# Sampled rows' convolution and layer norm taken out of the prompt's, and the cached rows' and bias copies' DMAs reordered

## What is computed

```python
def conformer_layer(x, conv_prev, g_pre, w_in, conv_w, conv_b, ln_g, ln_b, w_out, g_post):
    h = rms_norm(x, g_pre)
    a, b, z = jnp.split(h @ w_in, 3, axis=-1)
    glu = a * jax.nn.sigmoid(b)
    full = jnp.concatenate([conv_prev.astype(glu.dtype), glu], axis=1)
    c = lax.conv_general_dilated(full, conv_w[:, None, :].astype(glu.dtype), (1,), 'VALID',
                                 dimension_numbers=('NWC', 'WIO', 'NWC'),
                                 feature_group_count=D_INNER) + conv_b
    y = jax.nn.silu(layer_norm(c, ln_g, ln_b)) * jax.nn.silu(z)
    return x + rms_norm(y @ w_out, g_post), full[:, -(CONV_W - 1):]
```

## Time and profile before

| what | value |
| --- | --- |
| median of three runs | 1080.82 us |
| the profiled execution's own time | 1079.11 us |
| its span, first to last instruction | 1077.0 us |
| TensorE matmuls busy | 972.6 us, 90% |
| VectorE busy | 527.9 us, 49% |
| ScalarE busy | 419.5 us, 39% |
| GpSimd busy | 273.2 us, 25% |
| granted TensorE clock, mean | 0.972 of full speed |

### The profile page before, as it was taken

How to read it: one execution, slowest core, us unless ns; L and a number is a source line. 1 busy time by engine, 2 the same in 40 slices (tenths; PEclk the granted TensorE clock), 3 DMA queues, 4 the chain that set the end, 5 groups by cost and what they waited for, 6 DMA issues and landing times. The chain is left out here.

```text
span 1077.0 us, 16750 instructions
## 1 busy us (share of the span) xinstructions
PE 972.6 (90%) x6142; PEld 806.0 (75%) x6142; DVE 527.9 (49%) x1443; ACT 419.5 (39%) x864; POOL 273.2 (25%) x303
## 2 busy tenths in 40 slices
PE   2899999994699999998998999999999999899994
PEld 2799999652358878876998888788788887786652
DVE  3399999972331440223111445645545546445653
ACT  4466666432421121211222454555545536323320
POOL 0378888430130000002000132323233224200000
PEclk9999999997699999999998999999999999899997
DMA  8246333277301042035542212212211005703310
GB/s 222 64 115 180 97 97 107 104 288 258 105 8 46 40 147 69 23 83 128 138 93 55 49 36 60 59 40 60 59 41 40 21 1 125 211 20 119 120 50 29
DMA packets 153815, 97.12 MB, mean 90 GB/s; under 512 B 94004, under 2 KB 141780, under 8 KB 153655
## 3 DMA queue, kind: packets, MB, share of 16 engines
q1 hardware_dynamic: 142894, 81.52, 28.1%
q10 hardware_dynamic: 10105, 9.50, 2.7%
q0 software_dynamic: 736, 5.05, 1.2%
HBM read 87.22 MB, written 18.85 MB: 98 GB/s over the span
## 5 line engine op out<-in xcount | busy, mean ns | idle before, releaser
L1506 PE MATMUL psum<-arena 128*128 128x256 f32 (+3 forms) x928 | 195.2, 367 | 3.2 <-issue 2.6
L675 ACT ACTIVATE arena<-psum 128x512 f32<-128x512 f32 (+10 forms) x225 | 90.4, 453 | 260.4 <-PE psum L1826 72.5
L1506 PEld LDWEIGHTS psum<-arena 128*128 128x128 f32 (+2 forms) x928 | 160.5, 187 | 31.6 <-issue 10.1
L1526 PE MATMUL psum<-u_hi,tile_hi 128*128 128x288 f32 x512 | 158.2, 309 | 3.6 <-DVE kept L1282 3.6
L1527 PE MATMUL psum<-u_lo,tile_hi 128*128 128x288 f32 x512 | 152.3, 297 | 0.0
L1528 PE MATMUL psum<-u_hi,tile_lo 128*128 128x288 f32 x512 | 152.1, 297 | 0.0
L654 POOL TENSOR_SCALAR arena<-arena,kept 128x128 f32<-128x128 f32 (+3 forms) x128 | 76.6, 608 | 211.6 <-DVE kept L1354 211.6
L1158 DVE SCALAR_TENSOR_TENSOR psum<-arena,psum 128x512 f32<-128x512 f32 x168 | 125.7, 748 | 0.0
L1526 PE MATMUL psum<-h_hi,tile_hi 128*128 128x288 f32 x384 | 115.0, 299 | 10.0 <-ACT arena L675 4.3
L1527 PE MATMUL psum<-h_lo,tile_hi 128*128 128x288 f32 x384 | 114.6, 298 | 0.0
L1528 PE MATMUL psum<-h_hi,tile_lo 128*128 128x288 f32 x384 | 113.8, 296 | 0.0
(11 more groups left out here) (239 smaller groups left out, 1490.1 us busy)
## 6 DMA issues: line engine op xcount, KB each, us to landing
tile_whole<-in_b_w_in SPq DMA_DIRECT2D x64, 256.0 KB
tile_whole<-in_a_w_in SPq DMA_DIRECT2D x24, 512.0 KB
arena<-in_cmp_w SPq DMA_DIRECT2D x3, 2048.0 KB, 9.9
arena<-in_w_kv SPq DMA_DIRECT2D x6, 1024.0 KB, 7.7
bias_copies<-bias_line SPq DMA_DIRECT2D x4, 1280.0 KB
arena<-in_x_prompt SPq DMA_DIRECT2D x8, 512.0 KB, 16.2
arena<-in_a_w_out SPq DMA_DIRECT2D x4, 1024.0 KB, 29.3
arena<-bias_copies SPq DMA_DIRECT2D x16, 256.0 KB, 3.9
```

What stands on the lines that cost most here:

```text
L675: return nc.scalar.activation(out, in_, ACT.Copy, scale=scale)
L1506: ins = pe.matmul(out, l, r, start=(k == 0), stop=(k == len(pairs) - 1))
L1526: pe.matmul(out, w_hi[:, k], h, start=(k == 0), stop=False)
```

## The change

The sampled rows leave the prompt's chain. In the convolution VectorE does only the prompt's 22 taps and the final sum. Behind its adds GpSimd multiplies, for each block and each half of the sequences, the sliding windows by the 31 taps (16 products of 4 x 8 x 31 elements, three buffers), and VectorE sums each over the taps (16 reductions: 8 behind the centring, 8 behind the prompt's scaling). Then the bias, and the sampled rows' own mean, centring, square, variance, root, reciprocal, scaling and Silu for all blocks together. The prompt's multiplication by Silu(z) moves from GpSimd to VectorE. TensorE makes six of the eight mean matmuls before compression 0 and the other two behind it, at 512 columns. On SP the bias copies leave chunk C_OA, and at C_KV - 1 the order becomes: weights of compression 1, cached rows 12 to 15, the prompt's rows, the sampled rows, a wait for the sample's sums (whose buffers lie where the first kv chunks go). The strip bs is loaded at C_Q, its four copies on VectorE move behind q_ready. The bias copies are issued by ScalarE between the conv outputs' stores and the load of gpost_a. Three semaphores are merged into others. Core of the diff:

```diff
-CONV = 2 * W_ON + W_OFF + 2
+CONV = W_ON + 1
...
-                if c == C_OA:
-                    sp.wait_ge(S["line_out"], 16)
-                    for h0 in range(0, H, 4):
-                        sp.dma_start(bias_copies[h0:h0 + 4], bias_dram[h0:h0 + 4].unsqueeze(1).broadcast_to([4, P, NX])).then_inc(S["line_out"], 16)
+                if c == C_KV - 1:
+                    sp.wait_ge(S["cs_mm"], 2)
+                    sp.dma_start(w1_sb, I["cmp_w1"][1].rearrange("(j p) n -> p j n", p=P)).then_inc(S["w1_in"], 16)
+                    for n in range(12, 16):
+                        past_cmp(n)
                     sp.wait_ge(S["proj_a"], C_OA)
                     for t in range(4):
                         sp.dma_start(x_sb[:, t], I["x_prompt"][0, t * P:(t + 1) * P, :]).then_inc(x_in[t], 16)
-                if c == C_KV - 1:
-                    sp.wait_ge(S["cs_mm"], 2)
-                    sp.dma_start(w1_sb, I["cmp_w1"][1].rearrange("(j p) n -> p j n", p=P)).then_inc(S["w1_in"], 16)
                     sp.wait_ge(S["conv_step"], CONV * KD)
                     sp.dma_start(x_sb[0:NS, 4], I["x_sample"].rearrange("b t d -> (b t) d")).then_inc(x_in[4], 16)
+                    sp.wait_ge(S["sample_sums"], 2 * KD)
+                if c == C_Q:
                     sp.wait_ge(S["line_out"], 80)
                     sp.dma_start(bs, bass.AP(bias_copies.tensor, SEQ - 1 - PAST, [[P * NX, H], [NX - 1, DS], [1, KS]])).then_inc(S["bs_in"], 16)
-                    for n in range(12, 16):
-                        past_cmp(n)
...
-            pool.wait_ge(S["z_ready"], KD)
-            for m in range(KD):
-                pool.wait_ge(S["lns_ready"], m + 1)
-                pool.tensor_tensor(out=zA[:, m], in0=conv[:, m], in1=zA[:, m], op=ALU.mult).then_inc(S["y_ready"], 1)
+            pool.wait_ge(S["state_ready"], 16)
+            pool.wait_ge(S["glu_ready"], 3 * KD)
+            for n in range(2 * KD):
+                m, half = n // 2, n % 2
+                if n >= 3:
+                    pool.wait_ge(S["sample_sums"], n - 2)
+                new = glu_s[:, m, 4 * half:4 * half + 4]
+                windows = bass.AP(new.tensor, new.offset, [new.ap[0], [DS + W - 1, 4], [1, DS], [1, W]])
+                taps = vecT[:, m, 0:W].unsqueeze(1).unsqueeze(1).broadcast_to([P, 4, DS, W])
+                pool.tensor_tensor(out=sample_prod[:, n % 3].rearrange("p (b t) w -> p b t w", b=4), in0=windows, in1=taps,
+                                   op=ALU.mult).then_inc(S["sample_terms"], 1)
...
+            act.wait_ge(S["stat_mm"], 1 + KD)
+            act.wait_ge(S["centred"], KD + 1)
+            nc.scalar.activation(sg[:, 0, 0:KD * NS].rearrange("p (m n) -> p m n", m=KD), conv[:, :, SEQ:NT], ACT.Square).then_inc(S["sqd"], 1)
+            act.wait_ge(S["eps_ready"], 2)
+            nc.scalar.activation(rstd_ln[:, SEQ:NT], rstd_ln[:, SEQ:NT], ACT.Sqrt).then_inc(S["std_ready"], 1)
+            act.wait_ge(S["lnx_ready"], KD + 1)
+            for m in range(KD):
+                normed_silu(m, slice(SEQ, NT))
 
...
                 act.dma_start(O["conv_sample"][0, b, W - 1 - DS:W - 1], conv_out_s[DS * b:DS * b + DS]).then_inc(S["co_out"], 16)
+            act.wait_ge(S["line_out"], 16)
+            for h0 in range(0, H, 4):
+                act.dma_start(bias_copies[h0:h0 + 4], bias_dram[h0:h0 + 4].unsqueeze(1).broadcast_to([4, P, NX])).then_inc(S["line_out"], 16)
             act.dma_start(gpost_a, I["a_norm_post"][0:1, :].broadcast_to([P, D])).then_inc(S["gpost_in"], 16)
...
                     if w == 0:
                         V.tensor_scalar(acc_p, glu_p[:, m, 0:SEQ], tap, bias, ALU.mult, ALU.add).then_inc(S["conv_step"], 1)
-                        V.tensor_scalar(on, new[:, :, 0:DS], tap, bias, ALU.mult, ALU.add).then_inc(S["conv_step"], 1)
                     else:
-                        dve.wait_ge(S["conv_step"], before + tap_step(w - 1) + 1)
+                        dve.wait_ge(S["conv_step"], before + w)
                         V.scalar_tensor_tensor(out=acc_p, in0=glu_p[:, m, w:w + SEQ], scalar=tap, in1=acc_p,
                                                op0=ALU.mult, op1=ALU.add).then_inc(S["conv_step"], 1)
-                        dve.wait_ge(S["conv_step"], before + tap_step(w - 1) + 2)
-                        V.scalar_tensor_tensor(out=on, in0=new[:, :, w:w + DS], scalar=tap, in1=on,
-                                               op0=ALU.mult, op1=ALU.add).then_inc(S["conv_step"], 1)
-                    if w < W_OFF:
-                        far = W_ON + w
-                        tap = vecT[:, m, far:far + 1]
-                        if w == 0:
-                            V.tensor_scalar(late, new[:, :, far:far + DS], tap, None, ALU.mult).then_inc(S["conv_step"], 1)
-                        else:
-                            dve.wait_ge(S["conv_step"], before + tap_step(w - 1) + 3)
-                            V.scalar_tensor_tensor(out=kept_s if w == W_OFF - 1 else late, in0=new[:, :, far:far + DS], scalar=tap,
-                                                   in1=late, op0=ALU.mult, op1=ALU.add).then_inc(S["conv_step"], 1)
-                dve.wait_ge(S["conv_step"], before + CONV - 2)
-                V.tensor_tensor(out=kept_s, in0=kept_s, in1=on, op=ALU.add).then_inc(S["conv_step"], 1)
+                dve.wait_ge(S["conv_step"], before + W_ON)
                 dve.wait_ge(S["term_added"], (W_OFF - 1) * (m + 1))
                 V.tensor_tensor(out=conv[:, m, 0:SEQ], in0=acc_p, in1=tap_sum, op=ALU.add).then_inc(S["conv_step"], 1)
+
+            def sample_sum(n):
+                m, half = n // 2, n % 2
+                dve.wait_ge(S["sample_terms"], n + 1)
+                V.tensor_reduce(conv[:, m, SEQ + 32 * half:SEQ + 32 * half + 32], sample_prod[:, n % 3], AX.X,
+                                ALU.add).then_inc(S["sample_sums"], 1)
 
...
+            for n in range(KD):
+                sample_sum(n)
...
+            for n in range(KD, 2 * KD):
+                sample_sum(n)
+            conv_s = conv[:, :, SEQ:NT]
+            dve.wait_ge(S["sample_sums"], 2 * KD)
+            V.tensor_tensor(out=conv_s, in0=conv_s, in1=vecT[:, :, W + 1:W + 2].broadcast_to([P, KD, NS]), op=ALU.add).then_inc(S["sample_sums"], 1)
+            dve.wait_ge(S["z_ready"], KD)
+            for m in range(KD):
+                dve.wait_ge(S["lns_ready"], m + 1)
+                V.tensor_tensor(out=zA[:, m, 0:SEQ], in0=conv[:, m, 0:SEQ], in1=zA[:, m, 0:SEQ], op=ALU.mult).then_inc(S["y_ready"], 1)
 
...
+            dve.wait_ge(S["stat_mm"], KD + 2)
+            dve.wait_ge(S["sample_sums"], 2 * KD + 1)
+            V.tensor_tensor(out=conv_s, in0=conv_s, in1=pb(2, NS).unsqueeze(1).broadcast_to([P, KD, NS]),
+                            op=ALU.subtract).then_inc(S["centred"], 1)
+            dve.wait_ge(S["stat_mm"], KD + 3)
+            V.tensor_scalar(rstd_ln[:, SEQ:NT], pb(3, NS), EPS, None, ALU.add).then_inc(S["eps_ready"], 1)
+            dve.wait_ge(S["std_ready"], 2)
+            link(dve, V.reciprocal(rstd_ln[:, SEQ:NT], rstd_ln[:, SEQ:NT]))
+            dve.wait_ge(S["sqd"], KD + 1)
+            V.tensor_tensor(out=conv_s, in0=conv_s, in1=rstd_ln[:, SEQ:NT].unsqueeze(1).broadcast_to([P, KD, NS]),
+                            op=ALU.mult).then_inc(S["lnx_ready"], 1)
+            dve.wait_ge(S["lns_ready"], 2 * KD)
+            V.tensor_tensor(out=zA[:, :, SEQ:NT], in0=conv_s, in1=zA[:, :, SEQ:NT], op=ALU.mult).then_inc(S["y_ready"], 1)
...
+            pe.wait_ge(S["ones_ready"], 1)
+            pe.wait_ge(S["glu_ready"], 3 * KD)
+
+            def mean_part(m):
+                pe.wait_ge(S["conv_step"], CONV * (m + 1))
+                return pe.matmul(pb(0, SEQ), ones, conv[:, m, 0:SEQ], start=(m == 0), stop=(m == KD - 1))
+
+            for m in range(KD - 2):
+                mean_part(m)
             compress(0)
+            mean_part(KD - 2)
+            mean_part(KD - 1).then_inc(S["stat_mm"], 1)
             pe.wait_ge(S["w2_in"], 16 * 8)
             pe.wait_ge(S["hid_ready"], 2)
             product(pb(4, 480), ((w2_sb[:, 0, ht], hid[:, ht]) for ht in range(2))).then_inc(S["kc_mm"], 1)
...
+            pe.wait_ge(S["sample_sums"], 2 * KD + 1)
+            for m in range(KD):
+                ins = pe.matmul(pb(2, NS), ones, conv[:, m, SEQ:NT], start=(m == 0), stop=(m == KD - 1))
+            ins.then_inc(S["stat_mm"], 1)
             pe.wait_ge(S["hid_ready"], 4)
             pe.wait_ge(S["z_ready"], KD)
             for b in range(DB):
                 ins = product(pb(4, DB, P, p1=60)[:, b], ((hid[:, ht, 60 * b:60 * b + 60], w2_sb[:, 1, ht]) for ht in range(2)))
             ins.then_inc(S["vc_mm"], 1)
+            pe.wait_ge(S["sqd"], KD + 1)
+            for m in range(KD):
+                ins = pe.matmul(pb(3, NS), ones, sg[:, 0, m * NS:(m + 1) * NS], start=(m == 0), stop=(m == KD - 1))
+            ins.then_inc(S["stat_mm"], 1)
...
+                if t == 4:
```

(44 more changed lines are left out.)

34 lines of the change are left out of this document (15 added, 19 removed).

## The result

The changed kernel takes 1098.54 us (median of four runs, 1096.95 to 1101.69) against 1080.32 for the kernel before (1079.29 to 1080.88): a ratio of 1.0173, 95% interval 1.0148 to 1.0199. It is slower by some 18 us. The forecast was 1103 with a range of 1083 to 1114. The profiled execution took 1099.36 us, with a span of 1097.5, which is 20.5 above the span before; its granted clock is 0.960 in the mean.

What follows compares the result with a forecast made beforehand. TensorE, busy nine tenths or more except near 240 to 290 us, was taken as the bound. The profiled 1079.11 plus 22.6 (late third output tile and clock) plus 0.6 gave 1102.3, stated as 1103, range 1083 to 1114.

Steps and rivals of the forecast that it cites:

- Step 1: Prompt's convolution alone: VectorE blocks every 19 to 20 us instead of 22.32, compression 0 ends at 229.5; gain 2 us.
- Step 2: Cached rows: first load at 240 (bounds 233 and 250), compression 1 starts at 261, ends 22.7 us earlier.
- Step 3: Sampled rows' sums and own norm around compression 1: output rows start at 303.5, 17.4 us won up to there.
- the sign of step 3 being wrong: Output rows starting over 15 us behind compression 1's end; 13 us was forecast.
- Step 4: Bias copies on ScalarE hold it and the gain's load, landing at about 360; third output tile and clock: 22.6 us late.
- The spell at the lower clock: TensorE, empty some 36 us after two output tiles, loses 2.5 to 3 us more at half clock.
- Step 5: Small things: the sample's bias column copies moved to just before the head blocks, 0.6 us lost.
- the copies cost nothing on ScalarE: Rival: ScalarE's queue takes the bias copies at some 0.4 us each, gain's load overtakes them; 1064, faster; chance 0.14.
- only the issue blocks: Rival: gain lands with the queue's release at 340 to 344, third tile at 353.5; 1085; chance 0.10.
- The late chain: Rival: sampled rows' windows at double price, or cached rows starting at 250; 1112; chance 0.10.

Runs made afterwards that it cites:

- Experiment 5: The kernel before with only experiment 4's DMA order, sampled rows left in the prompt's convolution and norm: 1071.23 us, ratio 0.9902.
- experiment 6: Experiment 5 with GpSimd's two DRAM to DRAM copies moved behind its multiplications by Silu(z): 1057.52 us, ratio 0.9776.
- Experiment 8: experiment 4 with conv output transposes ahead of the sample's variance, ScalarE's sample root and Silus behind stores and gain's load: 1053.34 us, ratio 0.9741.
- experiments 1: The changed kernel with the four bias copies put back on SP, early, at chunk C_OA: 1071.07 us, ratio 0.9914.
- experiment 2: The changed kernel with the gain's load issued ahead of the four bias copies, still on ScalarE: 1084.15 us, ratio 1.0038.
- experiment 3: The changed kernel with the bias copies in the same place, 128 copies outermost instead of 4 heads: 1064.01 us, ratio 0.9856.
- experiment 4: The changed kernel with the bias copies in old shape on SP, late, behind the sampled rows' load: 1060.47 us, ratio 0.9820.
- experiment 7: The kernel before with the bias copies at their old place on SP, 128 copies outermost: 1070.36 us, ratio 0.9899.

## Why the prediction was right, and where it was off

The mechanism that the prediction called decisive is the one that the runs show. That the forecast, 1103, comes within 5 us of the median, 1098.54, is also owed to errors that cancel, as the steps tell.

**Step 1** held. The blocks follow each other in 19.0 to 20.0 us (19 to 20 predicted), the last block's sum starts at 213.69 (predicted 214), compression 0 ends at 228.23 (229.5).

**Step 2** had the right mechanism and one wrong term: I let the weights of compression 1 be held until 240, as three weight chunks were held for 26.36 us before. They are one DMA and their issue took 0.37 us; they landed 14.0 us later, at 242.3, but the cached loads behind them were issued without waiting for that. The first came at 232.75, which was my lower bound, and compression 1 started at 254.81, six us earlier than the 261 forecast; it ended at 283.28, 7.2 earlier. The distance between the two, taken as 21.1, was 22.1. Experiment 5 shows that GpSimd's copies do hold cached loads when they run at the same time (23.67 against 7.86 in experiment 6). Here they were issued at 209.70 and landed at 234.0, about when the cached loads began.

**Step 3** held in its prices: a product 2.1 us (2.3), a reduction 1.19 (1.2), the eight scalings of the prompt 4.91 (4.9). The last sum starts at 276.79 and ends 8 us before my 286. But the chain behind compression 1 was undersized: the output rows start 15.6 us behind its end, not 13, which is over the 15 that the prediction itself named as the sign of step 3 being wrong. I had given its links no prices of their own. One that I had left out is 3.9 us long: the sampled rows are centred at 285.74, but their square on ScalarE starts at 289.63, behind the copy of the product for the values (1.02 us from 288.71), which stands ahead of it in ScalarE's program. Experiment 8 measures what the chain costs against one that is off TensorE's path: 7 us at the second tile's end (329.56 against 322.62).

**Step 4**, which the prediction called the one that decides, is shown by experiments 1 to 4. Copies' issues: 33.3 forecast, 30.64 measured. Gain's issue: 12.5 and 12.99. Landing: 360, and 356.36. Start of the third tile: 369.3, and 364.33. The 5 us between are a balance: 7.2 too late at compression 1's end by step 2, 2.6 too short a chain by step 3, 1.8 too long a hold of ScalarE, 2.7 too short a time from there to the landing (10.7 us, not 8), and 1.3 too long from the landing to the third tile (8.0 us, not 9.3). The last has a wrong reason behind it. The prediction had the third tile wait for the second's bank; banks come back two tiles later, and what the third tile waited for were the transposes of the first tile, behind its normalised row at 362.51. The spell at the lower clock was priced at 2.8 us and took 1.5 at this place.

The rule weighed there, in the Trainium skill, "DMA: Bandwidth & Descriptors", section on issuing engines not being separate queues, that the time to initiate a DMA is usually small beside the transfer, doesn't hold for these copies: 30.64 us of ScalarE's time for four of them, where the transfer takes some 50 us (5.2 MB at 104 GB/s, an estimate). In their wide shape it does, 2.83 us beside landings of 7.9 to 18.5 us. The same page says in its rules for kernel authors that an outermost dimension below 16 confines a DMA to at most that many engines. The shares here agree: 0.26 beside the copies with 4 outermost, in the kernels before and after and in experiments 1, 2, 4, 5, 6 and 8, and 1.02 and 1.03 with 128, in experiments 3 and 7.

**Step 5** came out at about 0.8 us for 0.6.

**The sum.** 1102.3 by the steps, 1099.36 measured in the profiled execution. Up to the third tile the steps were 5 us too pessimistic, and in the clock there 1.3 more. Against that stand the 2.9 us of the longer spell near 514 us, which no step had, and some 0.5 of small things. Without that spell the sum would have been further off, so its closeness is in part luck.

**The rivals.** That the copies cost nothing on ScalarE is refuted by the trace, and its price of 1064 was 3.5 us too high for experiment 4, where they do cost nothing (1060.47): the output rows start 21.2 us earlier there (299.66 against 320.90), not 17.4. That experiment 3 took 1064.01 is no confirmation, since its gain still landed late. That only the issue blocks was priced at 1085, with the third tile at 353.5, and experiment 2, which comes near this case, took 1084.15, with the third tile at 353.38. The agreement is luck: the rival had ScalarE held until 340 to 344 by copies and gain, where experiment 2 holds it until 336.44 by the copies and then 7.05 us by the store, which wasn't in the price. The late chain, 1112, didn't come about.

What stays open: why the spell near 480 to 530 us is short in some executions and long in others; the last 0.8 us; and 1.7 us that experiment 3 loses to experiment 4 between 457 and 478 us.

## What to carry to other kernels

A DMA isn't always an instruction that its engine issues and forgets. Behind slow copies the issues of this kernel lasted up to 15.86 us each and held everything behind them on their engine. So price a moved DMA by the duration of its own issues in the trace, and put slow ones where the queue's next load is far from due. Look at the DMA share beside a slow transfer before you move it: 0.26 beside these copies was a matter of shape, and two lines were worth 10 us in the kernel before and some 34 in the changed one. And when a rewrite wins by ending something earlier, ask which transfer it thereby gets out of the way; here the order of two DMAs of GpSimd did as much as the rewrite, or more (13.7 us at the third tile from experiment 5 to 6, 8.5 from 5 to 4). Before two medians a few microseconds apart are compared, look whether both traces have the same spells at the lower clock.

## What the runs showed of the hardware that was not expected

Issues are held on ScalarE's queue as on SP's, for about the same times: 30.64 to 33.28 us for the four copies on ScalarE, 33.15 to 38.14 on SP. A store that is issued behind them is held too: 7.05 us for the first 512 KB of rows, against 0.34. Loads of SP are also held beside copies that GpSimd issued: eight cached loads for 23.67 us in experiment 5 against 7.86 in experiment 6, and in experiment 7 one load of 256 KB until 253.13, with the copies' landing at 253.3. And the same kernel can differ by some 5 us between executions on one chip, with its mean granted clock: 1060 us at 0.978 and 1055 at 0.982 in experiment 6, 1067.51 at 0.973 and 1061.39 at 0.977 in experiment 3.
